# Gate and up tiles of an FFN: high and low operand side by side in one matmul of 512 columns, the halves of the bank added at the evacuation

## The reference, cut to what matters

```python
hn = rmsnorm(h, norm_ffn_g[l])
gu = hn @ w_ffn_in[l]                       # 1024 -> 2 * 2816
h = h + (jax.nn.silu(gu[..., :FFN_HIDDEN]) * gu[..., FFN_HIDDEN:]) @ w_ffn_out[l]
```

## Time and profile before

| | us |
|---|---|
| median of 3 runs (1370.54 to 1374.43) | 1370.67 |
| the profiled execution | 1372.87 |
| its span in the profile | 1371.1 |
| busy in the span: PE, DVE, ACT | 1236.7, 808.0, 598.5 |
| mean granted TensorE clock | 0.951 of full speed |

### The profile page before, as it was taken

One profiled execution on the slowest core, in us unless ns is written; L12 is line 12 of the kernel. 1 busy time (PEld: TensorE's weight loads), 2 busy tenths in 40 slices (PEclk: granted clock), 3 DMA queues, 4 the chain that ended last, 5 costly groups with the idle time before them and its releaser, 6 DMA issues.

```text
span 1371.1 us, 22793 instructions
## 1 busy us (share of the span) xinstructions
PE 1236.7 (90%) x8638; PEld 1113.2 (81%) x8638; DVE 808.0 (59%) x1610; ACT 598.5 (44%) x1092; POOL 54.3 (4%) x51
## 2 busy tenths in 40 slices
PE   4999998988977899899999997999999979998986
PEld 4998897988967898888898886888677669987775
DVE  4655644567946855556566444455566546675763
ACT  4864345453121243433333333555455426554533
POOL 0000000001112000000000000000000000001000
PEclk9999999999988899999999997999999979989998
DMA  6453443442322344357885571122111114322110
GB/s 242 145 174 132 150 150 116 151 131 100 123 63 77 108 154 143 101 210 288 292 296 200 215 273 35 59 82 72 47 62 62 47 46 154 108 78 77 62 47 32
DMA packets 48397, 175.04 MB, mean 128 GB/s; under 512 B 5376, under 2 KB 6016, under 8 KB 47776
## 3 DMA queue, kind: packets, MB, share of 16 engines
q1 hardware_dynamic: 47664, 169.77, 36.6%
q0 software_dynamic: 624, 3.80, 0.8%
HBM read 172.50 MB, written 1.05 MB: 127 GB/s over the span
## 4 chain that ended last, share of the span: by engine, by line
PE 39%; issue 10%; DVE 6%; ACT 3%; POOL 0%; ACTq 0%; DVEq 0%; POOLq 0%
PE lin L1118 8%; PE lin L1120 8%; PE lin L1119 8%; PE score L1253 2%; PE o_bank L1275 2%; PE sum_bank L1216 2%; PE lin L1133 1%; PE lin L1134 1%; PE lin L1135 1%; PE score L1185 1%; DVE probs L1732 1%; ACT w_hi L1385 1%; PE sum_bank L1229 1%; DVE w_lo L1581 1%; PE lin L1169 1%
## 5 line engine op out<-in xcount | busy, mean ns | idle before, releaser
L1581 DVE TENSOR_TENSOR w_lo<-w_raw,w_hi 128x1024 fp32r<-128x1024 f32 (+1 forms) x272 | 328.5, 1214 | 233.6 <-ACT w_hi L1385 203.1
L1385 ACT CAST w_hi<-w_raw 128x1024 fp32r<-128x1024 f32 (+1 forms) x272 | 275.0, 1036 | 107.6 <-PE lin L1120 57.6
L1118 PE MATMUL lin<-XH,w_hi 128*128 128x256 f32 x448 | 131.1, 293 | 3.1 <-DVE w_lo L1581 3.1
L1119 PE MATMUL lin<-XL,w_hi 128*128 128x256 f32 x448 | 128.8, 287 | 0.0
L1120 PE MATMUL lin<-XH,w_lo 128*128 128x256 f32 x448 | 128.7, 287 | 0.0
L1118 PE MATMUL lin<-NH,w_hi 128*128 128x256 f32 x416 | 120.4, 289 | 1.4 <-DVE NL L1712 1.4
L1119 PE MATMUL lin<-NL,w_hi 128*128 128x256 f32 x416 | 117.6, 283 | 0.0
L1120 PE MATMUL lin<-NH,w_lo 128*128 128x256 f32 x416 | 117.5, 283 | 0.0
L1514 ACT ACTIVATE probs<-score,stat 128x512 f32<-128x512 f32 (+1 forms) x88 | 53.0, 607 | 115.0 <-DVE stat L1826 85.4
L1118 PEld LDWEIGHTS lin<-XH,w_hi 128*128 128x128 f32 x448 | 87.9, 196 | 7.0 <-issue 6.7
L1118 PEld LDWEIGHTS lin<-NH,w_hi 128*128 128x128 f32 x416 | 79.6, 191 | 14.5 <-issue 12.6
(11 more groups left out here) (368 smaller groups left out, 3195.3 us busy)
## 6 DMA issues: line engine op xcount, KB each, us to landing
w_raw<-in_ada SPq DMA_DIRECT2D x48, 512.0 KB, 5.4
w_raw<-in_w_out SPq DMA_DIRECT2D x32, 512.0 KB, 3.3
w_raw<-in_gate SPq DMA_DIRECT2D x22, 512.0 KB, 6.1
w_raw<-in_up SPq DMA_DIRECT2D x22, 512.0 KB, 3.7
w_raw<-in_ffn_out SPq DMA_DIRECT2D x16, 512.0 KB, 3.9
w_raw<-in_q SPq DMA_DIRECT2D x16, 512.0 KB, 3.4
w_raw<-in_z SPq DMA_DIRECT2D x16, 512.0 KB, 3.3
w_raw<-in_k SPq DMA_DIRECT2D x10, 512.0 KB, 3.3
```

The lines of the kernel that those rows point to most:

```text
L1118: nc.tensor.matmul(bank[:, 0:W], wh, moving(H, kk), start=first, stop=False)
L1119: nc.tensor.matmul(bank[:, 0:W], wh, moving(L, kk), start=False, stop=False)
L1385: scal.copy(w_hi[:, i % HL, 0:n], raw[:, tile["i"] % RAW, 0:n]).then_inc(w_hi_ready, 1)
L1581: vec.tensor_sub(w_lo[:, i % HL, 0:n], raw[:, tile["i"] % RAW, 0:n], w_hi[:, i % HL, 0:n].bitcast(F32)).then_inc(w_lo_ready, 1)
```

## The change

For gate and up tiles the two matmuls with the high weights become one of 512 columns: NH and NL are now two halves of one array, NHL, at the same place in memory, and the matmul's moving operand is slice k of both. The bank then holds in its first half high by high plus low by high, and in its second half high by low. The evacuation has to add them. ScalarE copies the second half of the bank to catb (two buffers in a slab that is free at that time), for gate and for up, as soon as PE has finished the tile; VectorE waits for that copy and adds it to the first half: for gate into rot, which is then multiplied by rstd in place; for up into catb, which takes the bank's place in the multiplication. Other stages keep their three matmuls.

```diff
--- before.py
+++ after.py
@@ -127,8 +127,10 @@
         HH, HLo = slab("HH", 7, [DT, T], F32R), slab("HLo", 8, [DT, T], F32R)
         GH, GL = slab("GH", 1, [DT, T], F32R), slab("GL", 2, [DT, T], F32R)
         hres = slab("hres", 3, [DT, T])
-        NH, NL = slab("NH", 5, [DT, T], F32R), slab("NL", 6, [DT, T], F32R)
+        NHL = slab("NHL", 5, [2, DT, T], F32R)
+        NH, NL = NHL[:, 0, :, :], NHL[:, 1, :, :]
         QX = slab("QX", 7, [DT, T])
+        catb = slab("catb", 0, [2, T], F32, SLAB // 2)
         CH, CL = slab("CH", 8, [DT, T], F32R), slab("CL", 9, [DT, T], F32R)
         FH, FL = slab("FH", 7, [FT, T], F32R), slab("FL", 10, [FT, T], F32R)
 
@@ -187,7 +189,7 @@
         rot_ready, roped = sem("rot_ready"), sem("roped")
         scored, maxed, exped, probs_ready = (sem(n) for n in ("scored", "maxed", "exped", "probs_ready"))
         transposed, pt_ready, pv_done, heads_out = (sem(n) for n in ("transposed", "pt_ready", "pv_done", "heads_out"))
-        gates_ready = sem("gates_ready")
+        gates_ready, cat_ready = sem("gates_ready"), sem("cat_ready")
         hg_qk, hg_scored, hg_taken, hg_att, hg_pv, hg_out = (sem(n) for n in
                                                              ("hg_qk", "hg_scored", "hg_taken", "hg_att", "hg_pv", "hg_out"))
         gate_used = sem("gate_used")
@@ -207,7 +209,7 @@
         tiles = []
         n_lin = [0]
         n_split = [0]
-        n_z = [0]
+        n_z, n_cat = [0], [0]
         rot_uses = []
         stage_last = {}
 
@@ -254,6 +256,9 @@
                 s["sq"] = new_sq(evac[3], 0, None, width // P, 1)
                 lin_sq[0] = s["sq"]
             s["later"] = defer[0]
+            if stage in ("gate", "up"):
+                n_cat[0] += 1
+                s["cat"] = n_cat[0]
             steps.append(("lin", s))
             lin_of[stage, t] = g
             if defer[0]:
@@ -1115,8 +1120,12 @@
                             pe.wait_ge(op_ready, op["ops"][kk])
                         if "gates" in s:
                             pe.wait_ge(gate_used, s["gates"] + kk + 1)
-                        nc.tensor.matmul(bank[:, 0:W], wh, moving(H, kk), start=first, stop=False)
-                        nc.tensor.matmul(bank[:, 0:W], wh, moving(L, kk), start=False, stop=False)
+                        if s["stage"] in ("gate", "up"):
+                            nc.tensor.matmul(bank[:, :].rearrange("p (two n) -> p two n", two=2), wh, NHL[:, :, kk, :],
+                                             start=first, stop=False)
+                        else:
+                            nc.tensor.matmul(bank[:, 0:W], wh, moving(H, kk), start=first, stop=False)
+                            nc.tensor.matmul(bank[:, 0:W], wh, moving(L, kk), start=False, stop=False)
                         last = nc.tensor.matmul(bank[:, 0:W], wl, moving(H, kk), start=False, stop=final)
                     if ks is None or ks[-1] == DT - 1:
                         last.then_inc(w_used, 1)
@@ -1432,6 +1441,11 @@
                 g, ev, t, W = s["g"], s["evac"], s["t"], s["w"]
                 bank = lin[g % NLIN]
                 free = lin_out[g % NLIN]
+                if "cat" in s:
+                    lin_done(act, s)
+                    if s["cat"] > 2:
+                        after_lin(act, g - 2)
+                    scal.copy(catb[:, s["cat"] % 2, :], bank[:, W:2 * W]).then_inc(cat_ready, 1)
                 if ev[0] == "act":
                     lin_done(act, s)
                     scal.copy(ev[1][:, t, 0:W], bank[:, 0:W]).then_inc(free, 1)
@@ -1644,12 +1658,18 @@
                     vec.tensor_mul(ev[1][:, t, :], bank[:, 0:W], r_of(ev[2], W)).then_inc(free, 1)
                 elif ev[0] == "silu":
                     rot_free(dve, s["slot"])
-                    vec.tensor_mul(rot[:, s["slot"] % 2, 0:W], bank[:, 0:W], r_of(ev[2], W)).then_inc(free, 1)
+                    r = rot[:, s["slot"] % 2, 0:W]
+                    dve.wait_ge(cat_ready, s["cat"])
+                    chain(vec.tensor_add(r, catb[:, s["cat"] % 2, :], bank[:, 0:W]))
+                    vec.tensor_mul(r, r, r_of(ev[2], W)).then_inc(free, 1)
                 elif ev[0] == "up":
+                    u = catb[:, s["cat"] % 2, :]
+                    dve.wait_ge(cat_ready, s["cat"])
+                    chain(vec.tensor_add(u, u, bank[:, 0:W]))
                     dve.wait_ge(silu_done, s["gate"])
                     r = rot[:, (s["slot"] - 1) % 2, 0:W]
                     chain(vec.tensor_mul(r, r, r_of(ev[2], W)))
-                    chain(vec.tensor_mul(r, r, bank[:, 0:W]))
+                    chain(vec.tensor_mul(r, r, u))
                     two_parts(FH[:, t, :], FL[:, t, :], r).then_inc(free, 1)
                 elif ev[0] == "zgate":
                     O_, H, L = ev[1:]
```

## The result

The changed kernel takes 1389.14 us (median of 4 runs, 1386.40 to 1391.38) where the kernel before takes 1372.25 on the same chip (4 runs, 1370.54 to 1374.43): ratio 1.0130, 95% interval 1.0108 to 1.0151, slower by 16.9 us. The forecast had the sign and less than half of the size: 1378.9, range 1373.0 to 1383.5. The profiled execution took 1388.56 us, span 1386.8.

The account below looks back on a forecast made before the run. PE was taken to bound the gate and up stage, until the change makes the ring longer than PE's pace. Terms +1.5 + 1.7 + 0 + 3.8 + 1.2 = +8.2 us on a median of 1370.67 gave 1378.9, range 1373 to 1383.5.

Parts of the forecast that it names:

- The bound: Gate and up stage: PE is saturated, with the loop through the other engines 0.5 us under the 6.94 us pair.
- the ring: Gate tile, copy, add, multiply, silu, w_hi, w_lo, next gate tile: 6.42 us before, 7.23 after, where PE needs 6.74.
- Start: Stage's beginning, to the multiply of gate t = 2: two adds delay w_lo and the multiply comes later, +1.5 us.
- Six pairs: Gate and up tile pairs t = 3 to 5 and 14 to 16: 6.94 us each become 7.23, +1.7 us.
- Eight pairs with squares: Middle pairs also carrying the context's squares: alternating between about 7.2 and 7.4 us against 7.27 before, so 0.
- Tail: From the multiply of t = 16 to ffn_out: VectorE's pair with two adds exceeds PE's, 39.1 against 35.29 us, +3.8.
- The clock: At ffn_out's start: idle of nearly 4 us drops PE to half speed, +1.2 us, bounds 0 and 2.
- rivals 1 and 2: Gate and up stage: first, PE stays the bound, 1366.4, 7%; second, gains and tail loss cancel, 1371.3, 13%.
- Rival 3: Gate and up stage: ScalarE's waits lengthen each hand-over 0.2 us, slow clock lasts 2 us more; +14, 1384.9, 10%.
- Rival 4: Merged matmul runs its halves in turn, 240 ns not 228; some 1.5 us more, inside the forecast's 70%.
- the 12 ns of a merge: Gate and up tiles: a 512-column matmul takes 228 ns against 2 x 120; 0.20 us a pair, 4.3 us in all.

Follow-up runs that it names:

- copy_no_add: The changed kernel with ScalarE's copies and their waits kept, both adds left out (that part of the product missing): 1370.44 us, ratio to before 1.0001.
- after_ahead: The changed kernel with ScalarE's splits one tile further ahead in the gate and up steps: 1371.69 us, ratio to before 0.9999.
- filler: The changed kernel with 30 unused matmuls in PE's idle ahead of ffn_out: 1382.17 us, ratio to before 1.0083.
- merge_only: The changed kernel without copy, wait and adds, merged matmul kept (bank's second half left out of the output): 1372.09 us, ratio to before 1.0002.
- before_idle: The kernel before, with VectorE repeating the last up tile's FH copy 8 times, delaying ffn_out by 2.6 us with PE idle: 1381.14 us, ratio 1.0067.
- idle_filled: The kernel before with ffn_out delayed 2.6 us by repeated FH copies, and 30 unused matmuls in that idle: 1372.66 us, ratio 1.0000.
- up_add_only: The changed kernel with the add kept at up and left out at gate, copies and waits kept: 1375.70 us, ratio to before 1.0029.
- gate_add_only: The changed kernel with the add kept at gate and left out at up, copies and waits kept: 1380.06 us, ratio to before 1.0065.
- reduce_ahead: The changed kernel with splits one tile further ahead and one VectorE reduction replacing copy and add: 1375.71 us, ratio to before 1.0021.

## Why the prediction was wrong, point by point

**The bound and the ring: right.** PE's 0.5 us of slack in a pair was the right thing to look at, and the ring of 7.23 us came at 7.29. copy_no_add, the two single adds and after_ahead show it from both sides.

**Start, +1.5: 1.76.** **Six pairs, +1.7: 2.47**, or 7.35 us each. **Eight pairs with squares, 0: 1.25**, or 7.48 each; the prediction saw that the up tile's w_lo could hold these back and let it cancel against 7.27, though it had "7.2 to 7.4" for them in the same sentence. For the six the reason is the hand-overs. 0.08 us was taken from silu, and 0.05 for w_lo to PE stands in no row; copy to add has 0.13 (690.46 + 0.37 to 690.96) and w_lo to PE 0.14 (694.55 to 694.69), 0.14 more in a turn than forecast (the turn shown has 0.07 of it back, since its silu starts 0.47 us after the multiply's start and not 0.54). In the eight a ring longer by the same 0.14, 7.37, would account for only 0.36 of the 1.25. In three of them (t = 5, 7 and 10) PE took the gate tile only 0.25 to 0.67 us after its w_lo was finished, so there not the ring alone but also the up tile, held back by its own w_lo, made the pair long; and the pair from t = 10 carries `ada_turn`: it took 7.68 us before, where 7.27 was used, and 7.86 after. Together these three terms are 5.5 us for a forecast of 3.2.

**Tail, +3.8: 3.67.** Pairs 16 to 20 were put at 7.89 and 3 x 6.75, the last at 5.61; the gate's adds start 7.86, 6.67, 6.84, 6.72 and 5.53 apart:

```profile
705.66 0.42 DVE L1663 TENSOR_TENSOR rot<-catb,lin 128x256 f32<-128x256 f32 x1 [0.57 <-ACT catb L1448]
713.52 0.41 DVE L1663 TENSOR_TENSOR rot<-catb,lin 128x256 f32<-128x256 f32 x1
720.19 0.41 DVE L1663 TENSOR_TENSOR rot<-catb,lin 128x256 f32<-128x256 f32 x1
727.03 0.41 DVE L1663 TENSOR_TENSOR rot<-catb,lin 128x256 f32<-128x256 f32 x1
733.75 0.41 DVE L1663 TENSOR_TENSOR rot<-catb,lin 128x256 f32<-128x256 f32 x1
739.28 0.41 DVE L1663 TENSOR_TENSOR rot<-catb,lin 128x256 f32<-128x256 f32 x1
```

The last five have no idle ahead of them: VectorE is the bound there. PE's idle of "almost 4" is 3.59.

**The clock, +1.2, bounds 0 and 2: some 4 to 7, with 6.5 the estimate from the half clock (147 less 130 us, at 0.38).** This is the step that failed. The drop to 1.2 GHz behind the idle was foreseen, and its direct price is 2.3 us (ffn_out's first tile), just over the upper bound: the earlier trace rows gave 0.8 and 1.7 for stretches in which PE had other waits as well. The missed part is the sentence "Everything behind ffn_out's start hangs on PE's progress there and moves as a block". It doesn't: the later stages' own half-clock stretches got longer (0.68 for 0.76 and 0.95 for 1.00), and filler gives them back; in the kernel before, the idle by itself cost 8.5 us. The bound was local because the rows were; nothing in the trace of before excluded an effect further on. *The Trainium skill, "TensorE: Matmul & The Clock Gate", in its part on the clock gate, puts the penalty of the ramp to the full clock at under 1% of a typical kernel's span, for modelling. That is said of the time until sustained matmuls reach the full clock, which no run here shows by itself; one idle in the middle cost about 0.5% here, a large part of what this change costs.*

Sum: 9.2 + 6.5 = 15.7, of a measured 16.9. The rest is within the noise of the half-clock stretches. In the distance to the forecast, 1389.14 against 1378.9, are 1.6 us more that are no matter of the mechanism: the forecast stood on a median before of 1370.67 (3 runs), and with the fourth it is 1372.25.

**The rivals.** Of rivals 1 and 2 nothing came, for the ring really was over PE's pace. Rival 3 (+14) was nearest in size and named "the slow clock lasts 2 us more", but its main price, 0.2 us on each hand-over, was again in the stage, where only some 2 us were missing. Rival 4 fell with merge_only, whose merged matmuls did shorten the stage. There PE's own pace could be read too: 40.74 / 6 = 6.79 us and 57.71 / 8 = 7.21, where 6.74 and 7.07 were put. Against 6.94 and 7.33 (58.60 / 8) before, a pair gained 0.15 and 0.11 us, not 0.20: the 12 ns of a merge were over-sized, so less than the 4.3 us would have come even to rival 1. Rival 3's own terms add up to 8.2 + 4.4 + 2 = 14.6, which its +14 rounds down.

## What to carry to other kernels

A matmul saved on a busy TensorE is worth only what the loop through the other engines allows: add that loop up link by link, with a measured time for each hand-over (0.08 to 0.14 us here), before counting columns. What the change adds should be looked at where it stands in program order; here one more tile of lookahead removed a loss of 9.3 us that fewer matmuls could not. And an idle of TensorE that pulls the clock down is priced by filling it with unused matmuls and measuring the whole program, not by the first slow stretch behind it.

## What was not expected of the hardware

- At one place, 3.67 us of idle cost 8.5 us more than the same delay filled with unused matmuls (before_idle, 1381.14, against idle_filled, 1372.66). 2.3 of them lie in the next tile, the rest in lower granted clock further on, up to 400 us later.
- Idles of 1.05 to 3.13 us at that place (up_add_only has 3.13, gate_add_only 2.63) left the half clock at 125 to 131 us in five of seven kernels, those of 3.5 us and more put it at 144 to 148. merge_only (1.16 idle, 136) and reduce_ahead (1.54, 139) share with the latter the 0.91 in the second stretch and the loss in the last; why is not settled.
- VectorE's reduction of 128x512 to 128x256 out of a bank took 0.69 us, against 0.42 for an addition with the same 256 results.
